# Expert-row gathers on more places, dot products between the key steps, and the gate table four chunks later, in a two-block transformer kernel

## The reference

```
def peer_ffn(u, w_q, sub_keys, u_tab, v_tab):
    q = (xt @ w_q).reshape(T, H, 2, PEER_DKEY // 2)
    s = jnp.einsum('thcd,hcnd->thcn', q, sub_keys)
    top_s, top_i = lax.top_k(s, K)
    cand = (top_s[:, :, 0, :, None] + top_s[:, :, 1, None, :]).reshape(T, H, K * K)
    cand_i = (top_i[:, :, 0, :, None] * PEER_NKEYS + top_i[:, :, 1, None, :]).reshape(T, H, K * K)
    best_s, best_j = lax.top_k(cand, K)
    expert = jnp.take_along_axis(cand_i, best_j, axis=-1)
    g = jax.nn.softmax(best_s, axis=-1)
    # for each group of 128 tokens: xc, its experts ec, its gates gc
    act = jax.nn.gelu(jnp.einsum('cd,chkd->chk', xc, u_tab[ec]))
    return jnp.einsum('chk,chkd->cd', gc * act, v_tab[ec])
```

## Time and profile before

| | us |
|---|---|
| median of three runs | 2440.09 (2438.62 to 2442.44) |
| the profiled execution | 2434.31 |
| its span, first to last instruction | 2432.6 |
| first stage of the expert layer, chunk 0 to the first output matmul | 1270.7 to 1901.6 |
| PE busy | 2370.5 (97%) |
| POOL busy | 1375.0 (57%) |
| DVE busy | 1782.6 (73%) |

### The profile page before, as it was taken

How to read it: one execution, slowest core, us unless ns; L and a number is a source line. 1 busy time by engine, 2 the same in 40 slices (tenths; PEclk the granted TensorE clock), 3 DMA queues, 4 the chain that set the end, 5 groups by cost and what they waited for, 6 DMA issues and landing times.

```text
span 2432.6 us, 32822 instructions
## 1 busy us (share of the span) xinstructions
PE 2370.5 (97%) x11991; PEld 1999.9 (82%) x11991; DVE 1782.6 (73%) x2987; ACT 1120.9 (46%) x2163; POOL 1375.0 (57%) x701
## 2 busy tenths in 40 slices
PE   8999999999999999999999999999998999999998
PEld 7766888888887666888889899999998888888887
DVE  5977685153235767564899969999973699899998
ACT  4246322223214555344543458888863333333333
POOL 4422455455432212343535767777777789888885
PEclk9999999999999999999999999999999999999999
DMA  4200222322521111232215568999999799999995
GB/s 158 86 18 18 97 94 82 108 104 76 186 88 53 36 36 53 99 109 84 108 61 163 185 229 296 353 350 355 351 357 406 267 365 381 371 364 359 360 360 211
DMA packets 152500, 476.60 MB, mean 196 GB/s; under 512 B 14768, under 2 KB 47920, under 8 KB 142000
## 3 DMA queue, kind: packets, MB, share of 16 engines
q1 hardware_dynamic: 115504, 340.69, 38.7%
q0 software_dynamic: 36864, 134.23, 15.2%
HBM read 422.44 MB, written 52.43 MB: 195 GB/s over the span
## 4 chain that ended last, share of the span: by engine, by line
PE 76%; DVE 14%; DMA 3%; POOL 3%; ACT 2%; issue 1%; SPq 0%; ACTq 0%; DVEq 0%; POOLq 0%
PE bank_pair L2372 20%; PE bank_pair L285 14%; PE bank_pair L286 14%; PE bank_pair L287 14%; DVE cacc L540 2%; PE bank_pair L2341 2%; DMA u_raw<-expert_u 2%; PE bank_pair L1426 1%; PE bank_pair L1463 1%; PE bank_pair L762 1%; POOL u_lo L2046 1%; POOL w_lo L254 1%; PE bank_pair L1479 1%; PE bank_pair L1435 1%; PE bank_pair L296 1%
## 5 line engine op out<-in xcount | busy, mean ns | idle before, releaser
L254 POOL TENSOR_TENSOR w_lo<-w_raw,w_hi 128x2048 fp32r<-128x2048 f32 (+3 forms) x94 | 411.1, 4373 | 577.8 <-ACT w_hi L249 577.8
L2046 POOL TENSOR_TENSOR u_lo<-u_raw,u_hi 128x1024 fp32r<-128x1024 f32 x128 | 315.2, 2464 | 181.5 <-ACT u_hi L2042 180.7
L285 PE MATMUL bank_pair<-uh,u_lo 128*128 128x384 f32 x1024 | 348.3, 340 | 15.5 <-POOL u_lo L2046 14.9
L286 PE MATMUL bank_pair<-ul,u_hi 128*128 128x384 f32 x1024 | 345.5, 337 | 0.0
L287 PE MATMUL bank_pair<-uh,u_hi 128*128 128x384 f32 x1024 | 345.3, 337 | 0.0
L2102 POOL TENSOR_TENSOR v_lo<-v_raw,v_hi 128x1024 fp32r<-128x1024 f32 x128 | 309.1, 2415 | 45.7 <-ACT v_hi L2098 44.0
L249 ACT ACTIVATE w_hi<-w_raw 128x2048 fp32r<-128x2048 f32 (+3 forms) x95 | 171.6, 1806 | 288.8 <-PE bank_pair L287 280.7
L2566 DVE TENSOR_TENSOR h_raw<-h_raw,g_in 128x384 f32<-128x384 f32 x128 | 255.2, 1994 | 41.9 <-DMA h_raw<-h_scratch 41.8
L2098 ACT ACTIVATE v_hi<-v_raw 128x1024 fp32r<-128x1024 f32 x128 | 135.7, 1060 | 268.9 <-PE bank_pair L2372 182.1
L285 PE MATMUL bank_pair<-xh,w_lo 128*128 128x512 f32 x624 | 245.4, 393 | 4.4 <-DVE sig L1715 2.0
L287 PE MATMUL bank_pair<-xh,w_hi 128*128 128x512 f32 x624 | 243.1, 390 | 0.0
(11 more groups left out here) (456 smaller groups left out, 5286.4 us busy)
## 6 DMA issues: line engine op xcount, KB each, us to landing
w_raw<-w_small SPq DMA_DIRECT2D x77, 1024.0 KB, 4.8
u_raw<-expert_u SPq DMA_DIRECT2D x128, 512.0 KB, 6.1
v_raw<-expert_v SPq DMA_DIRECT2D x128, 512.0 KB, 7.3
h_scratch<-h_act SPq DMA_DIRECT2D x128, 192.0 KB, 4.5
g_scratch<-stage SPq DMA_DIRECT2D x24, 1024.0 KB, 8.9
g_in<-g_scratch SPq DMA_DIRECT2D x16, 1536.0 KB, 12.6
h_raw<-h_scratch SPq DMA_DIRECT2D x128, 192.0 KB, 6.5
w_raw<-w_small SPq DMA_DIRECT2D x8, 768.0 KB, 4.1
```

The source lines that it names most:

```text
L254: pool.tensor_tensor(wl[g % 2][:, :n], raw[g % 2][:, :n], wh[g % 2][:, :n].bitcast(F32), ALU.subtract).then_inc(sem("lo_done"), 1)
L285: pe.matmul(out, al, bh, start=(k == 0), stop=False)
L286: pe.matmul(out, ah, bl, start=False, stop=False)
L2046: pool.tensor_tensor(u_lo[c % 2][:, :, :], u_raw[c % 4][:, :, :], u_hi[c % 2][:, :, :].bitcast(F32), ALU.subtract)\
```

## The change

Six edits, all in the expert layer:

- UG_EARLY, the number of gathers ahead of the table, goes from 4 to 12. Gather 0 still stands behind chunk 19. Before, gathers 1 to 3 followed behind chunks 20 to 22, and gathers 4 to 7 behind chunks 33 to 35. Now one stands behind each chunk of 19 to 25 (gathers 0 to 6) and of 27 to 30 (7 to 10), and 11 behind chunk 33. From there on the pace is the same, 4 in 3 chunks, and each chunk has 7 gathers more behind it than before, so that the last stands behind chunk 120 and not 125.
- Where buffers 4 to 6 were used by gathers 4 to 6 and 11 to 13, these go to three places of their own (`ug_first`), which lie where the scores were; the wait for all keys moves from gather 4 to gather 14.
- Four dots stand behind each of keys(1), (2) and (3), 12 in all; before, none stood before the first marks of the table.
- PRE goes from 36 to 40, so the table, its stores, `load_g(0)` and the first h and v loads stand four chunks later, and 16 chunks are left behind the table, not 20.
- The third turn goes from chunk 32 to 34.
- ACT's four copies to `top_f` stand behind chunks 14, 15, 16 and 17, one each, with a count each that keys(tt) waits for; before, all four stood behind chunk 14.

```diff
-        UG, UG_EARLY = 7, 4
+        UG, UG_EARLY = 7, 12
+        ug_first = [at(f"ug_first{i}", [P, D], scr(68 + 4 * i)) for i in range(3)]
+        def ug_of(j):
+            b = j % UG
+            return ug_first[b - 4] if b >= 4 and j < 2 * UG else ug[b]
...
-        PRE = 36
+        PRE = 40
-        TURN_AT = (25, 29, 32)
+        TURN_AT = (25, 29, 34)
...
-                return max(0, min(UG_EARLY, c - 18))
-            return min(P, UG_EARLY + (c - 32) * 4 // 3)
+                return max(0, min(UG, c - 18), min(UG_EARLY - 1, c - 19))
+            return min(P, UG_EARLY - 1 + (c - 32) * 4 // 3)
...
-            if j == UG_EARLY:
+            if j == 2 * UG:
                 pool.wait_ge(sem("pk_keys"), QT)
...
-                    for tt in range(QT):
-                        ins = act.activation(top_f[:, tt]..., top_i[:, tt, :, :, :], ACT.Copy)
-                    ins.then_inc(sem("pk_gexp"), 1)
+                if EXP_AT <= c < EXP_AT + QT:
+                    tt = c - EXP_AT
+                    act.activation(top_f[:, tt]..., top_i[:, tt, :, :, :], ACT.Copy)\
+                       .then_inc(sem("pk_gexp"), 1)
...
-                if tt == 0:
-                    dve.wait_ge(sem("pk_gexp"), 2)
+                dve.wait_ge(sem("pk_gexp"), 2 + tt)
...
                 keys(tt)
+                if tt:
+                    for j in range(4 * (tt - 1), 4 * tt):
+                        dot(j)
...
-            for j in range(UG_EARLY):
+            for j in range(UG_EARLY, dots_by(PRE - 2)):
                 dot(j)
-            done = UG_EARLY
+            done = dots_by(PRE - 2)
```

More of the change, by code:

```diff
@@ L2058, in gather_u @@
                 pool.wait_ge(sem("dot_done"), j - UG + 1)
-            pool.indirect_dma_start(ug[j % UG][:, :], None, u_rows, bass.IndirectOffsetOnAxis(idx_u[:, j:j + 1], 0))\
+            pool.indirect_dma_start(ug_of(j)[:, :], None, u_rows, bass.IndirectOffsetOnAxis(idx_u[:, j:j + 1], 0))\
                 .then_inc(sem(ug_loaded(j)[0]), 16)
@@ L2204, in block3_act @@
                     act.activation(best_e[:, :, :, :], best_e[:, :, :, :], ACT.Exp).then_inc(sem("pk_gexp"), 1)
-                    for tt in range(QT):
-                        ins = act.activation(top_f[:, tt].rearrange("p k j h -> p h j k"), top_i[:, tt, :, :, :], ACT.Copy)
-                    ins.then_inc(sem("pk_gexp"), 1)
+                if EXP_AT <= c < EXP_AT + QT:
+                    tt = c - EXP_AT
+                    act.activation(top_f[:, tt].rearrange("p k j h -> p h j k"), top_i[:, tt, :, :, :], ACT.Copy)\
+                       .then_inc(sem("pk_gexp"), 1)
                 if c in TURN_AT:
@@ L2522, in dot @@
                     dve.wait_ge(sem("x_turned"), 1)
-                rows = ug[j % UG]
+                rows = ug_of(j)
                 wait(dve, ug_loaded(j))
```

## The result

The changed kernel took 2448.22 us (median of eight runs, 2446.08 to 2451.84) where the kernel before took 2437.41 in the same series (eight runs, 2431.93 to 2442.44). The ratio is 1.0044, with an interval of 1.0032 to 1.0057: 0.44% slower, small but clear of the interval, where 2430.5 was forecast. The profiled execution took 2446.53 us, its span is 2444.8, so 12.2 more than the span before.

What follows compares the result with a forecast made beforehand. PE was taken as the bound, with about 98 us beside it, and transfers as bounding the end. Terms +2.3 + 1.0 + 0.3 - 13.2 = -9.6 us took the 2440.1 median to 2430.5, range 2423 to 2438.

Steps and rivals of the forecast that it cites:

- the sentence on the table: Table of 72 chunks, 362.5 us: neither shortened nor lengthened, since its three lists keep their pattern; priced at nothing.
- The signs that the prediction named as right: PE idle 4 us or more before chunk 20, low clock behind; chunk 17 stop under 1; end 70 to 72 us.
- Copies and gather 0: Chunks 15 to 25: spread copies bring PE 3.8 us ahead, but gather 0's wait for idx_u costs more; net +2.3 us.
- Seven gathers among the keys: POOL during the keys: one gather a chunk fits; two meetings with DVE's products are priced, +1.0 us.
- The two meetings taken at 0.5: Products of keys(2) and keys(3) each hold one POOL gather 1.9 us longer, priced at 0.5 us each.
- PRE = 40: Table's start: four chunks moved ahead, 0 changed in the sum; two gathers behind chunks 35 and 38 cost +0.3 us.
- The end: Behind the table: fewer transfers and no 7.04 us wait for weighted h; 4.0 us lost, not 17.2: -13.2.
- (1): Rival, chunks 15 to 20: the early gain of the spread copies stays, -4.8 us for +2.3, giving 2423.4; chance 0.12.
- (2): Rival, before the table: DVE's 16-bit work holds gathers, dots push keys(3) past the third turn; 2448 us, chance 0.06.
- (3): Rival, at the end: first h and v come too late, costing 6.5 us of the gain; 2437 us, chance 0.12.
- (4): Rival: the end stays at the transfers' rate and loses 9 us, 5 more than taken; 2435.5 us, chance 0.10.

## Why the prediction was wrong

**The failed step** is the sentence on the table: "It is neither shortened nor lengthened here, since its three lists keep their pattern." It priced the table at nothing, and the table took 22.2 us more, where all other terms together came to -9.5. The lists did not keep their pattern: DVE's went from three and one to two and two. The pace stayed 4 in 3; how it rounds at the new PRE was not asked. The order of DVE's instructions inside one period of the table, compared before and after, would have shown it. Restoring the dots in the changed kernel shortens its table by 21.5 us (384.68 to 363.22), and two and two in the kernel before lengthens its table by 21.5 (362.51 to 384.02): that cause is shown from both sides.

The signs that the prediction named as right all came: a stop of 5.29 us before chunk 20 with a low clock behind it, nothing over 1 us before chunk 17, an end of 71.44 us, no wait for weighted h. None of its signs looked at the table, so they could not tell that the forecast was failing there.

The other steps, each as measured:

- *Copies and gather 0, +2.3 forecast up to chunk 25.* PE ran ahead to 1355.69 at chunk 19 (forecast 1356.4), stood 5.29 us before chunk 20 (5.7) while POOL's gather waited 6.24 us for idx_u, and the start of chunk 21 was 1371.99, 3.1 later than before (2.9). One size was off: the clock stayed at 1.2 GHz for 6.8 us, not 3.4. And the changed kernel's stage began 0.65 us earlier, which no edit explains (in other versions it began up to 4 us later), so counted from chunk 0 it was 3.75 later. The chain of waits over it, of the changed kernel, in order of time, answers the earlier trace rows:

```profile
1361.35 0.24 DVE idx_u L2484
1361.59 0.28 issue
1361.87 1.13 POOL ug L2065
1363.00 0.04 issue
1363.04 2.36 POOL u_lo L2052
1365.39 0.04 issue
1365.44 0.69 PE bank_pair L285
```

- *Seven gathers among the keys, +1.0.* Chunks 21 to 34 took 59.63 us and 60.95 before (1368.89 to 1429.84): no cost of theirs can be seen, so the +3.3 of both terms up to chunk 35 was 1.8, or 2.4 counted from chunk 0. The two meetings taken at 0.5 did not occur: each of the seven took its 0.95 us. The Trainium skill's rule in "SBUF — State Buffer", "SBUF: two separate sides", by which seven meetings would cost 13 us, is not refuted: here none of the seven met a product. Two of POOL's splits did, and took 3.14 us and 2.82 where 2.40 is usual, without stopping PE; so did splits and a gather in the version that starts gathers at 21, as the row at 1394.92 shows. The first, begun in DVE's product of 1392.78 to 1395.07:

```profile
1394.19 3.14 POOL L2052 TENSOR_TENSOR u_lo<-u_raw,u_hi 128x1024 fp32r<-128x1024 f32 x1 [1.67 <-ACT u_hi L2048]
```

- *PRE = 40, +0.3.* +1.0, with 6.8 us at the low clock at the table's start, where it was 3.4; a part of this low clock lies inside the table's window in both.
- *The end, -13.2.* -12.3 (4.8 lost, 4.0 forecast; the four chunks moved away count as 16.64 here). The wait for weighted h is gone, as foreseen. That moving the table and moving the gathers need each other was only half seen: the text priced them as one sum of bytes.

That these terms came to -9.5 for -9.6 forecast is in part luck: +1.8 for +3.3, +1.0 for +0.3 and -12.3 for -13.2 are misses of -1.5, +0.7 and +0.9 that cancel, and 0.65 of the first is the early start of the stage.

Of the rivals, (1) could be had only by moving gather 0 (with it behind chunk 21, chunk 21 starts 4.1 earlier than before, counted from chunk 0), and (2), the slower one, gives nearly the measured time, 2448, by a mechanism that did not happen: right number, wrong place. (3) did not occur. (4) did not hold the end: 4.8 us were lost and not 9. In 20 slices one behind the other, 27 us, the rates above stand between 399 and 426 GB/s. The 358 of the Trainium skill, "DMA: Bandwidth & Descriptors", Specifications, which the page gives as one core's half of what two share, is exceeded by this trace of a kernel on one core. With the right table term the forecast for the profiled execution would have been 2424.7 + 22.2 = 2446.9, and 2446.53 was measured. For the median it would have been 2452.7, where 2448.22 was measured: 2.7 of the difference is the starting value, 2440.09 from three runs, where eight gave 2437.41. With the table's pattern kept, the forecast was 2430.5 and such a kernel measured 2426.67.

## What to carry to other kernels

When a loop's start moves, write out each engine's list for one whole period at the old and the new start and compare them row by row: a pace such as 4 in 3 can round another way, and the same work in another order can cost more than what the move brings. In a loop that is tight on two engines, ask of each movable instruction what stands behind it on its engine and who waits for that; here the right place for a dot was bounded from both sides, by `stage` and by the gathers. A stop that is filled pays only if the next wait in line doesn't end at a time of its own. And name a sign for every term of a forecast, the ones set to nothing above all.

## What the runs showed of the hardware

The low clock behind a stop had not one length. It lasted 3.4 us behind the 3.04 us stop of the earlier trace rows, and 6.8 behind the 5.29 us stop here, where it fell 1.8 us before PE started again. At the table's start, behind a stop of 4.0 us in both kernels, it lasted 3.4 us in the kernel before, where it fell 0.5 us after PE had started, and 6.8 in the changed kernel, where it fell 1.4 us before:

```profile
1455.77:1462.59 6.82, 5.42 (x18) 5.43 (x19) 2.42 (x3) 5.94 (x21) 2.87 (x3) 0.50 0.87 305
```

The versions with the dots restored alone and with the pace shifted, whose lists are alike up to chunk 33, show 6.8 and 3.4 there, in one execution each, so it does not look as if the edits decide it. What does is open.

The same 16-bit product of DVE took 4.38 us at 1349.00, begun while a split of POOL was in work, and 2.29 at 1369.62, begun 0.7 us after one had ended. At 1369.62 a gather was in work, begun 0.56 us before; neither took longer than alone (0.95 and 2.29), as far as POOL's spans can be trusted.

```profile
1349.00 4.38 DVE L2473 TENSOR_TENSOR one_hot<-one_hot,top_f 128x4096 bf16<-128x4096 bf16 x1
...
1369.62 2.29 DVE L2473 TENSOR_TENSOR one_hot<-one_hot,top_f 128x4096 bf16<-128x4096 bf16 x1
```
